# Two blocks of a small model: gate rows sent through DRAM in place of turns on TensorE, and column halves at the last down products and the tail

## The reference

```
mod = silu(c) @ mod_w[i] + mod_b[i]
sh0, sc0, g0, sh1, sc1, g1, sh2, sc2, g2 = split(mod, 9)
x = x + 0.5 * g0 * swiglu(modulate(rms_norm(x), sh0, sc0), w_gu, w_down)
x = x + g1 * mixer(modulate(rms_norm(x), sh1, sc1))       # layer 0: pooling, layer 1: differential attention
x = x + 0.5 * g2 * swiglu(modulate(rms_norm(x), sh2, sc2), w_gu, w_down)
...                                                        # after layer 1: a norm, then a third block without gates
return rms_norm(h + swiglu(...), norm_final_g)
```

## Time and profile before

| | |
|---|---|
| median of 3 runs | 1370.38 us (1368.65 to 1371.72) |
| the profiled execution's own time | 1369.79 us |
| its span | 1368.1 us |
| granted TensorE clock, mean | 0.996 of 2.4 GHz |
| PE busy | 97% |
| DVE / ACT / POOL busy | 69% / 47% / 11% |
| chain that ended last, by engine | PE 83%, DVE 7%, ACT 4%, DMA 3% |

### The profile page before, as it was taken

The page is one execution under the profiler, slowest core; times in us unless marked ns, Lnnn a source line. Parts: engine busy times, 40 slices in busy tenths (PEclk is TensorE's granted clock), DMA queues, the critical chain, the costliest instruction groups (busy, mean ns, idle before and its releaser), DMA issues.

```text
span 1368.1 us, 17819 instructions
## 1 busy us (share of the span) xinstructions
PE 1326.5 (97%) x6271; PEld 1079.2 (79%) x6271; DVE 947.8 (69%) x1125; ACT 644.0 (47%) x847; POOL 151.6 (11%) x227
## 2 busy tenths in 40 slices
PE   5999999999999999999999899999999999999997
PEld 3678887888888888888778788888887778888885
DVE  3788888779887788887677575465786556554452
ACT  3344334553333643335566643334665664643341
POOL 3110001200010100000231100010126000000000
PEclk9999999999999999999999999999999999999999
DMA  9999887499886698875543395555445444465540
GB/s 334 319 351 345 304 306 259 141 344 309 302 308 230 222 305 314 305 245 177 184 151 127 102 328 167 195 191 177 138 162 201 156 153 132 143 228 190 193 145 31
DMA packets 186070, 304.82 MB, mean 223 GB/s; under 512 B 8524, under 2 KB 134884, under 8 KB 185752
## 3 DMA queue, kind: packets, MB, share of 16 engines
q1 hardware_dynamic: 165432, 224.63, 48.8%
q0 software_dynamic: 20576, 79.37, 16.5%
HBM read 302.91 MB, written 1.05 MB: 222 GB/s over the span
## 4 chain that ended last, share of the span: by engine, by line
PE 83%; DVE 7%; ACT 4%; DMA 3%; issue 2%; POOL 1%; SPq 0%; POOLq 0%; DVEq 0%; ACTq 0%
PE ps L517 25%; PE ps L519 25%; PE ps L518 25%; DVE wlo L1893 2%; ACT whi L1292 2%; DVE arena L1934 2%; DMA raw<-in_ffn_w_gu 1%; DMA arena<-in_mod_w 1%; PE ps L599 1%; PE ps L635 1%; PE ps L626 1%; PE ps L948 1%; PE ps L672 1%; PE ps L970 1%; DMA raw<-in_ffn_w_down 1%
## 5 line engine op out<-in xcount | busy, mean ns | idle before, releaser
L1893 DVE TENSOR_TENSOR wlo<-raw,whi 128x2048 fp32r<-128x2048 f32 x212 | 482.6, 2299 | 97.0 <-ACT whi L1292 94.4
L517 PE MATMUL ps<-whi,nthi 128*128 128x512 f32 (+1 forms) x1264 | 505.8, 400 | 4.8 <-DVE ntlo L2217 2.8
L519 PE MATMUL ps<-whi,ntlo 128*128 128x512 f32 (+1 forms) x1264 | 493.1, 390 | 0.0
L518 PE MATMUL ps<-wlo,nthi 128*128 128x512 f32 (+1 forms) x1264 | 491.9, 389 | 0.0
L1292 ACT ACTIVATE whi<-raw 128x2048 fp32r<-128x2048 f32 x212 | 397.5, 1909 | 81.4 <-DMA raw<-in_ffn_w_gu 27.7
L517 PEld LDWEIGHTS ps<-whi,nthi 128*128 128x128 f32 x1264 | 238.2, 188 | 54.2 <-issue 5.9
L519 PEld LDWEIGHTS ps<-whi,ntlo 128*128 128x128 f32 x1264 | 238.0, 188 | 51.2
L518 PEld LDWEIGHTS ps<-wlo,nthi 128*128 128x128 f32 x1264 | 238.7, 189 | 45.2
L1934 DVE SCALAR_TENSOR_TENSOR arena<-arena,cact 128x512 f32<-128x512 f32 x238 | 178.7, 751 | 10.6 <-DMA arena<-in_mod_w 3.1
L517 PE MATMUL ps<-whi,hthi 128*128 128x512 f32 x440 | 172.7, 393 | 1.5 <-DVE htlo L1984 1.0
L519 PE MATMUL ps<-whi,htlo 128*128 128x512 f32 x440 | 171.6, 390 | 0.0
(11 more groups left out here) (276 smaller groups left out, 871.9 us busy)
## 6 DMA issues: line engine op xcount, KB each, us to landing
raw<-in_ffn_w_gu SPq DMA_DIRECT2D x176, 512.0 KB, 5.2
arena<-in_mod_w POOLq DMA_DIRECT2D x72, 1024.0 KB, 6.8
raw<-in_ffn_w_down SPq DMA_DIRECT2D x88, 512.0 KB, 5.5
raw<-in_w_in SPq DMA_DIRECT2D x44, 512.0 KB, 4.6
raw<-in_w_gate_up SPq DMA_DIRECT2D x44, 512.0 KB, 4.8
raw<-in_diff_w_qkv SPq DMA_DIRECT2D x24, 512.0 KB, 4.6
raw<-in_w_down SPq DMA_DIRECT2D x22, 512.0 KB, 5.8
raw<-in_diff_w_o SPq DMA_DIRECT2D x8, 512.0 KB, 4.1
```

Of the source, the lines that this page charges most:

```text
L517: pe.matmul(o, hi, wh, start=start, stop=False)
L518: pe.matmul(o, hi, wl, start=False, stop=False)
L519: return pe.matmul(o, lo, wh, start=False, stop=stop)
L1893: v.tensor_tensor(wlo[:, s * PIECE:(s + 1) * PIECE], raw[:, r * PIECE:(r + 1) * PIECE], hi, ALU.subtract).then_inc(w_lo, 1)
```

## The change

The gate rows leave PE and ACT's copies. ACT sends the 8 columns of a gate (128 partitions by 8 values) to a row of an internal DRAM tensor with a DMA, waits for it later, and fetches the row back, broadcast to all partitions, into `gate` with a second DMA. In an FFN the columns are first halved into a small tile `gcol`. An FFN's send stands behind the loop over the blocks, its fetch behind the next block's silus; pooling and attention have places of their own.

In every FFN the second column half of d9 of tile 0 moves behind `turn_one(0, A)`. In ffn 4, d10 of tile 1 is signalled in halves, and the end of tile 1 is done in halves of 512 columns, with the scaling shared by DVE and ACT.

```diff
@@ PE, ffn
-                down_block(d9, 1, 0, False, False)
+                down_block(d9, 1, 0, False, False, halves=(0,))
                 if MOD_NINTH[f]:
                     turn_chunk()
                 turn_one(0, A)
-                if gated is not None:
-                    gate_rows(gated, (B, M))
+                down_block(d9, 1, 0, False, False, halves=(1,))
                 d10 = down_piece()
                 pe.wait_ge(drained[T], n.seen(T))
                 down_block(d10, 0, 0, False, True).then_inc(sums_done, 1)
...
-                down_block(d10, 0, 1, False, True).then_inc(w_used, 1)
+                if f == 4:
+                    down_block(d10, 0, 1, False, True, halves=(0,)).then_inc(last_half, 1)
+                    down_block(d10, 0, 1, False, True, halves=(1,)).then_inc(w_used, 1)
+                else:
+                    down_block(d10, 0, 1, False, True).then_inc(w_used, 1)
@@ PE, pool and diff_attention
-                        pe.wait_ge(pcol_ready, 1)
-                        gate_row(pcol, 0, M)
-                gate_row(pcol, 1, M)
-                gate_row(mod_cols(1, 5), 0, M)
-                gate_row(mod_cols(1, 5), 1, T)
@@ ACT
+            def send_gate(i, cols_, halved=False):
+                if halved:
+                    s = n.next("halved")
+                    if i:
+                        act.wait_ge(gate_sent, 16 * i)
+                    nc.scalar.activation(gcol[:, :], cols_, ACT.Copy, scale=0.5).then_inc(gate_scaled, 1)
+                    act.wait_ge(gate_scaled, s.at + 1)
+                    cols_ = gcol[:, :]
+                act.dma_start(gate_rows[i].rearrange("(j p) -> p j", p=P), cols_,
+                              allow_slow_non_contiguous=True).then_inc(gate_sent, 16)
+
+            def fetch_gate(i):
+                act.wait_ge(gate_sent, 16 * (i + 1))
+                if i:
+                    act.wait_ge(gate_used, 2 * i)
+                act.dma_start(gate[:, :], broadcast(gate_rows[i], D)).then_inc(gate_landed, 16)
@@ ACT, ffn
-                ffn_steps(f)
+                known = ffn_steps(f)
+                if gated is not None:
+                    act.wait_ge(drained[M], known)
+                    send_gate(FFN_GATE[f], gated, halved=True)
                 split(3)
                 inner()
+                if gated is not None:
+                    fetch_gate(FFN_GATE[f])
                 split(1)
                 inner_hi(1)
...
-                if gated:
-                    gate_rows(0.5, (B, M))
@@ ACT, pool and diff_attention
                 scaled_band(0)
+                act.wait_ge(pcol_ready, 1)
+                send_gate(POOL_GATE, pcol)
                 n.next(M)
                 squares(1)
                 scaled_band(1)
                 pass_by(A, B, T)
+                fetch_gate(POOL_GATE)
...
+                send_gate(ATT_GATE, mod_cols(1, 5))
                 blocks_head(j, (g_cols, shift), START["qkv"], keep)
...
                 mixed(5)
+                fetch_gate(ATT_GATE)
                 weights(7)
@@ DVE, joined
-                if gated:
+                if gated is not None:
                     if t == 0:
-                        for b in gated:
-                            dve.wait_ge(drained[b], n.seen(b))
+                        dve.wait_ge(gate_landed, 16 * (gated + 1))
                     v.tensor_tensor(xnt[:, t, :], o, gate[:, :], ALU.mult).then_inc(sums_read[t], 1)
@@ the end: ACT, DVE, POOL, SP
-            squares(1)
+            for h in range(2):
+                act.wait_ge(x_ready, q + h + 1)
+                nc.scalar.activation(ps[:, 2 + h, :], x[:, 1, h * BLK:(h + 1) * BLK], ACT.Square,
+                                     accum_out=(ss, ssg)[h][:, 1:2]).then_inc(sq_done, 1)
+            act.wait_ge(rstd_done, 2 * TB + n.seen("norms") + 2)
+            nc.scalar.activation(xnt[:, 1, 0:BLK], xnt[:, 1, 0:BLK], ACT.Copy, scale=rstd[:, 1:2]).then_inc(y_ready, 1)
...
+            for h in range(2):
+                c = slice(h * BLK, (h + 1) * BLK)
+                v.tensor_tensor(x[:, 1, c], x[:, 1, c], ps[:, 2 + h, :], ALU.add).then_inc(x_ready, 1)
+            for h in range(2):
+                v.tensor_tensor(xnt[:, 1, c], x[:, 1, c], row[:, c], ALU.mult).then_inc(z_row, 1)
+            v.tensor_scalar(xnt[:, 1, BLK:D], xnt[:, 1, BLK:D], rstd[:, 1:2], None, ALU.mult).then_inc(y_half, 1)
...
+            g.tensor_scalar(ss[:, 1:2], ssg[:, 1:2], 1.0 / D, ss[:, 1:2], ALU.mult, ALU.add).then_inc(rstd_v, 1)
...
+            sp.dma_start(out[0, P:2 * P, BLK:D], xnt[:, 1, BLK:D]).then_inc(out_done, 16)
+            sp.dma_start(out[0, P:2 * P, 0:BLK], xnt[:, 1, 0:BLK]).then_inc(out_done, 16)
```

More of the change, by code:

```diff
@@ L493, in _ @@
             ffn(4)
[L495 to L498, removed]
+            sp.wait_ge(y_ready, 1)
+            sp.dma_start(out[0, 0:P, :], xnt[:, 0, :]).then_inc(out_done, 16)
+            sp.wait_ge(y_half, 1)
+            sp.dma_start(out[0, P:2 * P, BLK:D], xnt[:, 1, BLK:D]).then_inc(out_done, 16)
+            sp.wait_ge(y_ready, 2)
+            sp.dma_start(out[0, P:2 * P, 0:BLK], xnt[:, 1, 0:BLK]).then_inc(out_done, 16)
+            sp.wait_ge(out_done, 16 * (TB + 1))
         @block.tensor
@@ L802, in ffn_steps, with ffn @@
                     step(0)
-            def ffn(f, gated):
+            def ffn(f):
                 if f == 0:
@@ L1268, in _ @@
             keep_awake(T, 20)
-            ffn(0, mod_cols(0, 2))
+            ffn(0)
             pool()
@@ L1273, in _ @@
             keep_awake(T, 26)
-            ffn(1, mod_cols(0, 8))
-            ffn(2, mod_cols(1, 2))
+            ffn(1)
+            ffn(2)
             diff_attention()
-            ffn(3, mod_cols(1, 8))
+            ffn(3)
             second_mix()
-            ffn(4, None)
+            ffn(4)
         @block.scalar
@@ L1698, in diff_attention @@
                 turned_half_hi(1, 1, B)
-                row = n.next("gate")
-                act.wait_ge(gate_used, 2 * row.at)
-                gate_row(0, M, 1.0)
-                gate_row(1, T, 1.0)
             def second_mix(j, g_cols):
@@ L1875, in _ @@
             j = join(*norm, (2, 0, 1, 0), silu_at=1)
-            at = ffn(4, j, norm, False)
+            at = ffn(4, j, norm, None)
             squares(0)
@@ L2162, in ffn, with joined @@
                     add_chunk()
-                if gated:
-                    pass_by(M, B)
-            def joined(t, last, gated=(M, B)):
+            def joined(t, last, gated=None):
                 s = n.next(f"sums {t}")
@@ L2224, in pool_join @@
                 v.engine_nop().then_inc(g_ready, 1)
-                joined(0, last, (M, M))
-                joined(1, last, (M, M))
+                joined(0, last, POOL_GATE)
+                joined(1, last, POOL_GATE)
                 dve.wait_ge(rstd_done, n.next("rstd").at + 1)
@@ L2234, in pool_join, with join @@
                 return j, (scol[:, :], shift)
-            def join(g_cols, shift, splits, last, gated=(M, B), scale=None, tail=False):
+            def join(g_cols, shift, splits, last, gated=None, scale=None, tail=False):
                 j = n.next("join").at
@@ L2264, in final_join @@
                 v.engine_nop().then_inc(g_ready, 1)
-                joined(0, last)
+                joined(0, last, FFN_GATE[3])
                 gained(0)
@@ L2274, in final_join @@
                 x_lo(0)
-                joined(1, last)
+                joined(1, last, FFN_GATE[3])
                 gained(1)
@@ L2730, in _ @@
             ffn(4, j, norm, False)
-            for t in range(TB):
-                joined(t, START["end"] - 1, None)
-                if t == 0:
-                    n.next(B)
-                    product(1, B)
-                    one_lo(0, 1)
-                    dve.wait_ge(row_landed, 32)
-                dve.wait_ge(rstd_done, n.next("rstd").at + 1)
-                v.scalar_tensor_tensor(xnt[:, t, :], x[:, t, :], rstd[:, t:t + 1], row, ALU.mult, ALU.mult)\
-                 .then_inc(y_ready, 1)
+            joined(0, START["end"] - 1, None)
+            n.next(B)
+            product(1, B)
+            one_lo(0, 1)
+            dve.wait_ge(row_landed, 32)
+            dve.wait_ge(rstd_done, n.next("rstd").at + 1)
+            v.scalar_tensor_tensor(xnt[:, 0, :], x[:, 0, :], rstd[:, 0:1], row, ALU.mult, ALU.mult)\
+             .then_inc(y_ready, 1)
+            done = n.next("x").at
+            for h in range(2):
+                if h == 0:
+                    dve.wait_ge(last_half, 1)
+                else:
+                    dve.wait_ge(w_used, START["end"] + 1)
+                c = slice(h * BLK, (h + 1) * BLK)
+                v.tensor_tensor(x[:, 1, c], x[:, 1, c], ps[:, 2 + h, :], ALU.add).then_inc(x_ready, 1)
+            for h in range(2):
+                dve.wait_ge(x_ready, done + h + 1)
+                c = slice(h * BLK, (h + 1) * BLK)
```

(4 more changed lines are left out.)

81 lines of the change are left out of this document (37 added, 44 removed).

## The result

The changed kernel takes 1386.06 us (median; 1385.01 to 1393.37) beside 1371.05 for the kernel before on the same chip. The ratio is 1.0122, with a 95% interval of 1.0099 to 1.0144: it is slower by some 15 us, where 5 us faster had been forecast. Its profiled execution took 1386.54 us, with a span of 1384.9.

A forecast was written before the change was run, and what follows sets the result against it. PE, busy 97% of the span, was taken as the bound. 1.35 + 1.35 + 1.19 + 1.18 + 1.5 − 2 × 0.37 − 1.2 = 4.6 us gained, so 1365.4 us, range 1362.4 to 1368.2.

The forecast's parts named there:

- ACT's new work: Each FFN's send ahead of three weight splits: copy, hop and issue, 0.8 us, of which 0.37 falls on PE.
- ffn0: First FFN: gate saving of 1.35 us not counted; send and fetch delay its last chunk, losing 1.2 us, ends 0 and 4.7.
- Nor does ACT wait for the sent row: At an FFN's fetch: the send stands some 10 us before, so ACT isn't held; no cost charged.
- Rival A: Sends hold ACT until landing and the kernel is slower: 1376.3 us at a delay of 4.5 us; chance 0.09.
- ffn3: FFN gate rows leave PE between d9 and d10: 1.19 us saved, with no charge for the send.
- ffn4 and tail: Moved d9 half fills PE's wait for the low part, 1.18 us; halved work behind the last matmul saves 1.5 us.
- pooling and attention: Gate rows there lie beside or within PE's waits for DVE's low parts, so removing them gains nothing.
- ffn1 and ffn2: Gate rows leave PE ahead of d10: 1.35 us saved in each, less 0.37 for the send's delay.
- the charge of 0.37 us for ScalarE's delay: Behind the FFN loop: the uncovered part of the send's 0.8 us makes PE wait ahead of the turn, 0.37 us, charged twice.
- the three signs of the forecast's failure: Forecast is wrong if a send's issue lasts over 1 us, `joined` waits for a fetch, or ffn0's wait doesn't grow.

The follow-up runs named there:

- the reads alone: Kernel before plus six unused transfers reading a 4 KB DRAM row into 128 x 8 columns in four-byte pieces: 1370.43 us, ratio 0.9995.
- The fifth experiment: Changed kernel with ScalarE issuing the fetch in the four FFNs behind the next split and high part, not ahead of them: 1385.97 us, ratio 1.0106.

## Why the prediction was wrong

**The step that failed** is in "ACT's new work". It bounded the send by two rows, an issue of 0.43 us and a landing of 4.1 us, asked which of them holds ScalarE, and chose the issue. That was right: 0.38 us for 1,024 pieces. But the landing of 4.1 us was taken from a load, a transfer that reads DRAM in short runs, and the reads alone confirm that such a one harms nobody. The send writes; it took 8.6 us at the least, and what it does to other transfers was in no term at all. The sum priced a delay of the next transfers only for the fetch, and only in ffn0 (0.6 us, at most 3.9). By the runs the missing term is 21 us.

**"Nor does ACT wait for the sent row"** rested on 10 us between send and fetch, and fell with the landing: 12.3 us in ffn1. The fifth experiment shows no cost of this by itself that is clear of the noise.

**Rival A** named the right suspect, single values of four bytes, and the wrong way for them to act. It asked whether the issue holds ScalarE. Its price at a landing of 4.1 us, 1376.3, still lies 10 us under the time.

**The rest of the sum held.** With longer runs the changed kernel takes 1365.02 us, where 1365.4 was forecast. Step by step, from the table of stages: ffn3 −1.28 (forecast −1.19), ffn4 and tail −2.64 (−2.68), pooling and attention 0.0 (0). ffn1 and ffn2 gave 1.48 and 1.11 where 0.98 was forecast: the charge of 0.37 us for ScalarE's delay was too high, since no wait ahead of the turn shows there. ffn0 lost 0.17 instead of 1.2. Against these stand 1.42 in the second mix, by the clock as said above. So it is partly luck that 1365.02 lies so near 1365.4: the other stages gained 1.7 us more than forecast, and the clock took 1.4 of them.

**None of the three signs of the forecast's failure** came: issues stayed under 1 us, `joined` waited for no fetch, and ffn0's wait did grow, to 3.73 us where some 3 had been forecast, though for another reason. They ask about the issue, the fetched row and a wait that had been forecast anyway, so none of them could show what the sends did to other transfers.

The two rules of the Trainium skill that the prediction weighed come out apart. That a non-contiguous last dimension becomes one descriptor per element ("DMA: Bandwidth & Descriptors", Rules for kernel authors) agrees with the count: the queue of the sends has 7,104 packets in the changed kernel and 1,728 with 32-byte runs, six times 896 fewer. That the sequencer stays until the descriptors are made ("Perfetto Trace Analysis", DMA Instruction — HWDGE) hardly shows: 1,024 pieces were issued in 0.37 to 0.38 us, 512 in 0.37, 128 in 0.33 and eight in 0.29, too little to matter. A third rule was overlooked: the Trainium skill, "DMA: Bandwidth & Descriptors", Specifications, says that below 512 bytes the engines read, modify and write. The runs agree only in part, since runs of 32 bytes and four-byte writes far apart cost nothing.

## What to carry to other kernels

Ask of a small transfer not only how long its issue holds an engine and when it lands, but what it does to the transfers beside it; and take the bound from a row of the same direction. Columns that go to DRAM number by number are better turned first, so that each write is a run: runs of 32 bytes were enough here, though in another order. Numbers 16 bytes apart cost nothing either; a kernel that fetches such a row was not tried. Where weights set the time, work that is taken from the busiest engine may come back as a wait, as argued above.

## What the runs showed of the hardware

- 4 KB written as 1,024 numbers side by side all but stopped the core's other transfers for some 8 us (48 GB/s over 8.8 us, 259 before). As reads, or as writes 16 or 512 bytes apart, they cost nothing; 512 numbers side by side are as slow as 1,024.
- Issuing a transfer of 1,024 pieces took 0.37 to 0.38 us, of 512 pieces 0.37, of 128 pieces 0.33.
- After waits of 3.5 to 3.7 us TensorE ran at half its clock for 2.9 us or more; after waits of 1.3 and 1.85 us it did not, and after one of 1.98 us it did in the kernel before and did not in the changed one.
- VectorE turned four blocks of 32 x 32 into other partitions in 0.84 us.
